# Two layers of a hybrid decoder: page numbers clamped once, and the merged stage planned with other step durations

## The chip, the cores and the metric

The kernel runs on one core of a Trainium2 chip. The metric is the device time of one execution in microseconds (us). A core has TensorE (PE, matmuls), VectorE (DVE), ScalarE (ACT) and GpSimd (POOL), each with its own in-order instruction queue, and SyncE (SP), which computes nothing: its queue issues all DMAs of this kernel. Engines hand work to each other by semaphores that are counted up and waited for.

## The reference

One inference step of two decoder layers, for a prompt of 512 tokens and 8 sample sequences of one new token each with 2048 past tokens in a paged cache. Per layer:

```
h = rms_norm(x); proj = h @ w_in
q, kv_rows, win_rows, gates = nsa_project(proj[..., :NSA_PROJ], pos)     # rotary, sigmoid gates
o_nsa  = gates-weighted sum of three attentions: compressed blocks, top-16 selected blocks of 64, window of 512
o_rwkv = rwkv_time_mix(proj[..., NSA_PROJ:], state)                      # scan S = S*w + (S a) b + v k
x = x + rms_norm(concat(o_nsa, o_rwkv) @ w_out)
x = x + rms_norm(conv_ffn(rms_norm(x)))                                  # up 1024->5632, width-3 conv, gelu, down
```

For the samples, the keys and values of the past come from `cache_kv` through `page_table`: `page_table[b, i]` is the physical page (128 tokens) of logical page i of sequence b, 16 pages per sequence, 160 pages in the pool. Everything is float32.

## The kernel before

Both layers run in one hardware loop (`Fori(0, DEPTH)`) on every engine. A layer has dense parts (w_in at the start; w_out, w_up and w_down at the end), in which 128x1024 weight chunks pass through a ring of three (`ring`, line 740), ACT and DVE split each into a high and a low part (lines 1297 and 1632), and PE multiplies three products per block (lines 826 to 828). Between them lies a short stage for rotary, compression and the samples' RWKV step, and then the *merged stage*, which runs from about 270 to 745 us of layer 1.

The merged stage interleaves three independent jobs: the RWKV scan of the prompt in four super-chunks (`rwkv`), the prompt's attention in 32 units (`att`), and the samples' attention (`sample`). The order is not written by hand. `rwkv_threads`, `att_thread`, `sample_thread` and `load_thread` (lines 158 to 327) list every step with its engine, a duration in us and what it depends on; `placed` (line 330) simulates the engines and puts the steps in one list, choosing the step that can begin first, less a favour for its thread; `merged_order` (line 362) varies the favours at random in 4000 rounds and keeps the order with the shortest simulated span. `HOP` is what a dependence adds, `LANDING` the same for a load. The result is the list `PAIRED` (line 403), and PE, DVE and ACT each walk through that same list and emit their part of each step. An engine's queue is in order, so a step that waits holds up all behind it.

The samples' past comes in 36 *units* per layer through three slots of 1 MB (`load_unit`, lines 688 to 707). Units 0 to 15 are compression rows (8 pages each), 16 and 17 window keys, 18 and 19 window values (one DMA each), 20 to 27 selected keys and 28 to 35 selected values (16 pages each). Unit u may be loaded when PE has used unit u-3 (`u_used`). For each unit SP loads the page numbers from SBUF into registers (line 704, with a check that each lies within the pool), and then issues one DMA per page, with an address worked out from the register (line 707). PE's users of the units are line 1145 (compression), 1176 (window keys, step `win_k`), 1184 (`sel_k`), 1220 (`win_v`) and 1229 (`sel_v`).

At the very start, SP issues consts, pages and x (lines 712 to 714, semaphore `const_ok`), and right behind them the layer's parameters (`par`, shift, lora; lines 732 to 734) and the first three weight chunks. DVE, ACT, PE and POOL wait for `const_ok`. POOL then clears 8192 columns of the arena (line 1559); DVE scales `onesblk` (line 1597), waits for the parameters and scales a part of `par` (line 1643), and after the norm writes `hm` (line 1648).

Of the kernel before, what the change touches and what calls it, by code (L numbers as in the profile page):

```python
# [150 lines left out]
HOP, LANDING = 0.25, 2.5  # L151
# [6 lines left out]
def rwkv_threads():  # L158

    front, back, side, tail = [], [], [], []  # L160
    for sc in range(SEQ // SC):
        def into(thread):
            def put(name, engine, us, *after):
                deps = [("rwkv", sc + a[0], a[1]) for a in after if 0 <= sc + a[0] < SEQ // SC]
                thread.append((("rwkv", sc, name), engine, us, deps))
            return put

        here, ago, next_ = (lambda *names: [(0, n) for n in names]), (lambda n: (-1, n)), (lambda n: (1, n))
        put = into(front)
        put("mix", "DVE", 0.5, ago("rkv"))  # L170
        put("tanh", "ACT", 1.0, *here("mix"))
        put("mixlow", "DVE", 1.8, *here("mix"))
        put("squares", "DVE", 1.5, *here("mixlow"))
        put("lora_w", "PE", 1.7, *here("tanh"))
        put("sigw", "ACT", 1.5, *here("lora_w"))
        put("decay", "DVE", 2.4, *here("sigw"))
        put("lora_a", "PE", 1.7, *here("sigw"))
        put("exps", "ACT", 2.2, *here("decay"))
        put("siga", "ACT", 1.5, *here("lora_a"))
        put("kknorm", "PE", 1.0, *here("squares", "siga"))  # L180
        put("keymix", "DVE", 1.5, *here("kknorm"))
        put("root", "ACT", 0.8, *here("kknorm"))
        put("keys", "DVE", 5.3, *here("root"))

        put = into(back)
        put("scaled", "DVE", 3.1, ago(("solve", 1)), *here("exps", "keys"))
        for c in range(2):
            put(("pairb", c), "PE", 1.4, ago(("state", 1)), ago(("yout", 1)), *here("scaled"))
        put(("maskb", 0), "DVE", 0.7, *here(("pairb", 0)))
        put(("pairk", 0), "PE", 1.4, *here(("maskb", 0)))  # L190
        put(("maskb", 1), "DVE", 0.7, *here(("pairb", 1)))
        put("nmm", "PE", 1.4, ago("ycopy"), *here("scaled"))
        put(("pairk", 1), "PE", 1.4, *here(("maskb", 1)))
        put("w0", "DVE", 1.5, *here("nmm"))
        put("zz", "DVE", 1.8, *here(("maskb", 1)))
        for c in range(2):
            put(("maskk", c), "DVE", 0.7, *here(("pairk", c)))
        for lv in range(1, LEVELS):
            put(("inv", lv), "PE", 1.4, *here(("add", lv - 1) if lv > 1 else "w0", ("maskb", 1)))
            put(("qcopy", lv), "ACT", 0.6, *here(("inv", lv)))  # L200
            put(("dbl", lv), "PE", 2.0 if lv < LEVELS - 1 else 1.0, *here(("qcopy", lv), "zz", ("maskk", 1)))
            put(("add", lv), "DVE", 1.5 if lv < LEVELS - 1 else 0.8, *here(("dbl", lv)))
        for c in range(2):
            put(("rhs", c), "PE", 2.0, *here(("state", 0) if c else ("add", LEVELS - 1), ("tmcopy", 2)))
            put(("rhcopy", c), "ACT", 0.4, *here(("rhs", c)))
            put(("solve", c), "PE", 0.8, *here(("rhcopy", c)))
            put(("ucopy", c), "ACT", 0.4, *here(("solve", c)))
            put(("advance", c), "PE", 1.5, *here(("ucopy", c)))
            put(("state", c), "DVE", 1.2, *here(("advance", c)))
            put(("yout", c), "PE", 1.7, *here(("ucopy", c)))  # L210

        put = into(side)
        put("rkprep", "DVE", 1.5, *here("scaled"))
        for n in range(3):
            put(("tm", n), "PE", 1.3, *([ago("vrec")] if n == 0 else here(("tmcopy", n - 1))), *here("scaled"))
            put(("tmcopy", n), "ACT", 0.6, *here(("tm", n)))
        put("glora", "PE", 1.2, *here(("tmcopy", 2)))
        put("gcopy", "ACT", 0.6, ago("out"), *here("glora"))
        put("rknorm", "PE", 1.1, *here("gcopy", "rkprep"))
        put("rkv", "DVE", 0.7, ago("out"), *here("rknorm"))  # L220
# [4 lines left out]
        put("msub", "DVE", 1.5, *here("mean"))
        put("var", "PE", 1.3, *here("msub"))
        put("vrec", "DVE", 4.2, *here("var"))
        put("vroot", "ACT", 0.8, *here("vrec"))
        put("out", "DVE", 3.5, *here("vroot"))
    return [front, back, side, tail]  # L230


def att_thread():

    out = []
    for t in range(NQ):
        w = t + 1

        def put(n, name, engine, us, *after):
            out.append((("att", n, name), engine, us, [("att",) + a for a in after]))  # L240

        first, last = HEADS * t, HEADS * (t + 1) - 1
        put(t, "cs", "PE", 1.4, *([(first - 1, "evac")] if t else []))
        if t:
            put(first - 1, "values", "PE", 0.2 + 0.35 * t, (first - 1, "evac"))
        put(t, "cmask", "DVE", 1.8, (t, "cs"))
        if t:
            put(t - 1, "heads", "DVE", 0.8, (first - 1, "values"))
        put(t, "cexp", "ACT", 0.6, (t, "cmask"))
        put(t, "cweigh", "DVE", 1.6, (t, "cexp"))  # L250
        put(t, "cturn", "PE", 1.2, (t, "cweigh"))
        put(t, "cdone", "DVE", 1.5, (t, "cturn"))
# [9 lines left out]
    put(last, "values", "PE", 0.2 + 0.35 * w, (last, "evac"))  # L262
    put(NQ - 1, "heads", "DVE", 0.8, (last, "values"))
    return out


def sample_thread():
# [6 lines left out]
    put("qz", 0, "DVE", 1.8)  # L274
    for b in range(DEC):
        for q in range(8):
            put("chunks", (b, q), "PE", 1.1, 2 * b + q // 4)
        for name, engine, us in (("cmp_part", "ACT", 0.7), ("cmp_sum", "DVE", 1.8), ("cmp_tanh", "ACT", 0.5),
                                 ("cmp_h", "DVE", 0.4), ("cmp_out", "PE", 0.9), ("cmp_keep", "DVE", 0.7)):
            put(name, b, engine, us)  # L280
    for name, engine, us in (("c_scores", "PE", 1.5), ("c_max", "DVE", 0.4), ("c_exp", "ACT", 0.6), ("c_weigh", "DVE", 1.0),
                             ("c_same", "PE", 0.8), ("c_impt", "DVE", 0.8), ("c_imp", "PE", 4.2), ("c_top", "DVE", 4.0)):
        put(name, 0, engine, us)
    for h in range(2):
        put("win_new", h, "DVE", 0.3, U_WK + h)
        put("win_k", h, "PE", 1.5, U_WK + h)
    for kind in ("win", "sel"):
        if kind == "sel":
            for h in range(2):
                for b in range(QD):  # L290
                    put("sel_k", QD * h + b, "PE", 0.7, U_SK + QD * h + b)
                put("sel_bias", h, "DVE", 0.8)
            put("sel_new", 0, "PE", 0.6)
        for name, engine, us in (("_max", "DVE", 0.6), ("_max_t", "PE", 0.3), ("_max_r", "DVE", 0.7), ("_max_b", "PE", 0.2),
                                 ("_nm", "DVE", 0.3), ("_exp", "ACT", 1.4), ("_den", "PE", 0.2), ("_rr", "DVE", 1.4)):
# [23 lines left out]
def load_thread(smp):  # L319
# [6 lines left out]
    return [(("load", u, "unit"), "SP", 0.6 * UNIT_DMAS[u] + 0.5, [last_use[u - USLOT]] if u >= USLOT else [])  # L326
# [104 lines left out]
def build(nc, I, O):  # L431
    with ExitStack() as ctx:
# [194 lines left out]
        const_ok = ctx.enter_context(nc.semaphore("const_ok"))  # L627
        ones_ok = ctx.enter_context(nc.semaphore("ones_ok"))
# [59 lines left out]
        def load_unit(eng, kind, l, u):  # L688
# [12 lines left out]
            else:  # L701
# [3 lines left out]
                pages[0:1, first:first + n], engines=[kind], min_val=0, max_val=N_POOL - 1)  # L705
# [5 lines left out]
        def _(sp):  # L711
# [17 lines left out]

            with sp.Fori(0, DEPTH) as l:  # L730
# [860 lines left out]
        def _(dve):  # L1591
# [5 lines left out]
            o.do(v.tensor_scalar(onesblk[:], blk, 1.0 / HD, None, MUL))  # L1597
            with dve.Fori(0, DEPTH) as _l:
# [653 lines left out]
```

## Time and profile before

| what | value |
|---|---|
| median of 3 runs | 2500.74 us (2498.71 to 2502.35) |
| the profiled execution's own time | 2501.68 us |
| its span | 2499.9 us |
| busy share of PE, DVE, ACT, POOL | 84%, 50%, 29%, 7% |
| mean granted PE clock | 0.892 |
| 0 to 270 us | dense w_in, then rotary and the samples' RWKV |
| 270 to 745 us | merged stage of layer 1 |
| 745 to 1249 us | dense w_out, w_up, w_down |
| 1249 to 2500 us | layer 2, merged stage at 1515 to 1991 us |

Times in the profile are us from the span's start unless marked ns. "SPq", "DVEq" and so on are the queues' own instructions, which do not count as busy. The granted clock is 1.0 at PE's higher clock level. In a row of a timeline, what stands in brackets is the engine's idle time before the row and what ended it. In the chain of waits, each piece is what the end of the execution was waiting for at that time.

### The profile page before, as it was taken

What the parts mean: (1) busy time and instruction counts of PE and PEld (TensorE: products, weight loads), DVE (VectorE), ACT (ScalarE), POOL (GpSimd) and SP (SyncE); (2) the same over time, 40 slices, a digit from 0 to 9 for tenths busy, and PEclk for the clock granted to TensorE, in tenths of its full rate; (3) what the DMA queues carried; (4) which work ended last, traced back from release to release, by engine and by line L of the source; (5) the groups of instructions that cost most, each with busy time, mean ns of one, the idle gap of its engine ahead of it and who ended that gap; (6) DMA issues with size and microseconds to landing.
All of it is one profiled execution on the core that took longest, in us unless ns stands there. A gap on an engine that the chain in (4) does not pass through costs nothing.

```text
span 2499.9 us, 56131 instructions
## 1 busy us (share of the span) xinstructions
PE 2088.2 (84%) x22574; PEld 1898.2 (76%) x22574; DVE 1251.8 (50%) x2079; ACT 719.3 (29%) x1336; POOL 165.1 (7%) x233
## 2 busy tenths in 40 slices
PE   6996698887768799999669967988878688999995
PEld 5995687755647699999669856776556477999995
DVE  4223767774743644452332236677757435444523
ACT  3221222332323322242132212323423223222421
POOL 1000120100100010000010001101101000010000
PEclk8988798888989799999879977988888798999997
DMA  3264232122222122223123632322222221222232
GB/s 122 93 138 145 71 100 87 54 71 76 59 82 86 51 93 91 90 84 101 47 79 94 147 127 86 93 80 62 72 74 59 89 71 60 93 93 90 89 93 72
DMA packets 172781, 216.53 MB, mean 87 GB/s; under 512 B 39009, under 2 KB 138594, under 8 KB 171106
## 3 DMA queue, kind: packets, MB, share of 16 engines
q1 hardware_dynamic: 172514, 212.87, 28.5%
q8 instruction: 180, 2.95, 0.5%
q14 instruction: 87, 0.71, 0.1%
HBM read 204.57 MB, written 16.59 MB: 88 GB/s over the span
## 4 chain that ended last, share of the span: by engine, by line
PE 59%; DVE 20%; SPq 11%; issue 6%; ACT 3%; DMA 1%; DVEq 0%; ACTq 0%
PE ps L826 15%; PE ps L828 15%; PE ps L827 15%; SPq L707 7%; SPq L704 3%; PE ps L1145 3%; PE ps L894 1%; DVE arena L1675 1%; DVE smp L1940 1%; PE ps L867 1%; DVE arena L1898 1%; DVE x L2081 1%; DVE arena L1905 1%; DVE hf_lo L1639 1%; PE ps L953 1%
## 5 line engine op out<-in xcount | busy, mean ns | idle before, releaser
L826 PE MATMUL ps<-hm_hi,ring_hi 128*128 128x260 f32 x2432 | 694.8, 286 | 35.7 <-DVE hm_lo L1639 35.7
L828 PE MATMUL ps<-hm_hi,ring_lo 128*128 128x260 f32 x2432 | 692.6, 285 | 0.0
L827 PE MATMUL ps<-hm_lo,ring_hi 128*128 128x260 f32 x2432 | 690.5, 284 | 0.0
L1632 DVE TENSOR_TENSOR ring_lo<-ring,ring_hi 128x1024 fp32r<-128x1024 f32 x200 | 244.8, 1225 | 696.9 <-ACT ring_hi L1297 696.2
L826 PEld LDWEIGHTS ps<-hm_hi,ring_hi 128*128 128x128 f32 x2432 | 464.0, 191 | 39.5 <-issue 39.5
L827 PEld LDWEIGHTS ps<-hm_lo,ring_hi 128*128 128x128 f32 x2432 | 463.6, 191 | 0.0
L828 PEld LDWEIGHTS ps<-hm_hi,ring_lo 128*128 128x128 f32 x2432 | 463.3, 191 | 0.0
L1297 ACT ACTIVATE ring_hi<-ring 128x1024 fp32r<-128x1024 f32 x200 | 211.8, 1060 | 681.3 <-PE ps L828 673.9
L826 PE MATMUL ps<-hf_hi,ring_hi 128*128 128x260 f32 x704 | 202.2, 287 | 8.8 <-DVE hf_lo L1639 8.2
L828 PE MATMUL ps<-hf_hi,ring_lo 128*128 128x260 f32 x704 | 200.7, 285 | 0.0
L827 PE MATMUL ps<-hf_lo,ring_hi 128*128 128x260 f32 x704 | 200.4, 285 | 0.0
L826 PEld LDWEIGHTS ps<-hf_hi,ring_hi 128*128 128x128 f32 x704 | 134.5, 191 | 11.4 <-issue 10.6
L828 PEld LDWEIGHTS ps<-hf_hi,ring_lo 128*128 128x128 f32 x704 | 134.5, 191 | 0.0
L827 PEld LDWEIGHTS ps<-hf_lo,ring_hi 128*128 128x128 f32 x704 | 134.4, 191 | 0.0
L1456 ACT ACTIVATE arena<-ps,arena 128x128 f32<-128x128 f32 (+3 forms) x128 | 66.5, 525 | 174.5 <-DVEq L428 173.8
L1577 POOL TENSOR_TENSOR arena<-arena,cst 128x256 f32<-128x256 f32 x80 | 63.3, 812 | 679.4 <-DVEq L428 475.4
L1462 ACT ACTIVATE arena<-ps 128x256 f32<-128x256 f32 (+3 forms) x64 | 45.2, 707 | 189.6 <-PE ps L1120 188.5
L843 PE MATMUL ps<-arena,ones 128*32 128x130 f32 x512 | 32.7, 353 | 58.5 <-ACT arena L1307 51.5
L1583 POOL COPY arena<-arena 128x2 f32<-128x2 f32 x44 | 28.5, 648 | 786.3 <-ACTq L428 786.3
L1030 PE MATMUL ps<-nsa 64*64 64x64 f32 x1280 | 78.9, 231 | 0.3 <-ACTq L428 0.2
L1030 PEld LDWEIGHTS ps<-nsa 64*64 64x64 f32 x1280 | 71.6, 141 | 8.1 <-issue 6.0
L1120 PE MATMUL ps<-cst,arena 128*128 128x128 f32 x320 | 57.3, 320 | 24.0 <-DVEq L428 23.9
(376 smaller groups left out, 3295.9 us busy)
## 6 DMA issues: line engine op xcount, KB each, us to landing
ring<-in_w SPq DMA_DIRECT2D x202, 512.0 KB, 3.6
arena<-in_kv_cmp SPq DMA_DIRECT2D x96, 128.0 KB, 2.2
extra<-in_kv_cmp SPq DMA_DIRECT2D x80, 128.0 KB, 2.1
slot<-in_kv_cmp SPq DMA_DIRECT2D x80, 128.0 KB, 2.2
out_win_old<-in_win SPq DMA_DIRECT2D x16, 511.0 KB, 9.3
slot<-in_k_sel SPq DMA_DIRECT2D x96, 64.0 KB, 1.9
arena<-in_k_sel SPq DMA_DIRECT2D x96, 64.0 KB, 1.9
extra<-in_v_sel SPq DMA_DIRECT2D x96, 64.0 KB, 1.9
```

What stands on the lines that cost most here:

```text
L704: _, regs = nc.values_load_multi_w_load_instructions(pages[0:1, first:first + n], engines=[kind], min_val=0, max_val=N_POOL - 1)
L707: eng.dma_start(dst[:, i, :], src[l * N_POOL + r]).then_inc(done, 16)
L826: mmul(out, wh, hi[:, k, cols], start=(k == 0), stop=False)
L827: mmul(out, wh, lo[:, k, cols], start=False, stop=False)
L828: last = mmul(out, wl, hi[:, k, cols], start=False, stop=(ci == len(chunks) - 1 and k == k1 - 1))
L1030: last = mmul(ps[r, 0, cj * CH:(cj + 1) * CH], qq[r, c, j, :], zz[r, c, j, :], start=True, stop=True)
L1120: last = nc.tensor.transpose(ps[:, 4 + g, k * P:(k + 1) * P], pp[:, g, k * P:(k + 1) * P], ident)
L1145: last = mmul(out, w1s[:, c, k, :], slot[:, :, c, k, :], start=(k == 0), stop=(k == STRIDE // 2 - 1))
L1297: A(ring_hi[:, n % RING_HI, :], ring[:, n % RING, :], ACT.Copy).then_inc(S["w_hi"], 1)
L1456: o.go(A(pp[:, g, 0:w], ps[:, 4 + g, 0:w], ACT.Exp, bias=nm[:, g:g + 1], accum_out=sums[:, g:g + 1]))
L1577: o.go(g.tensor_tensor(mm[:, lv % 2, c * RJ:(c + 1) * RJ, :], gb[:, c, :, 0, :], m, ALU.mult))
L1632: v.tensor_tensor(ring_lo[:, n % RING, :], r, ring_hi[:, n % RING_HI, :], SUB).then_inc(S["w_lo"], 1)
```

## The change

Three things change. The page numbers are limited to 0..159 by one instruction of DVE at the start, `pages_ok` tells SP so, SP waits for it ahead of the layer loop, and the loads of page numbers go without the check. The planner's step durations, the hop per engine and the load's cost get other values. The instructions of the steps stay as they are; their order is made anew from these values.

```diff
-HOP, LANDING = 0.25, 2.5
+HOP, LANDING = {"PE": 0.13, "DVE": 0.0, "ACT": 0.0}, 2.5
...
-        put("lora_w", "PE", 1.7, *here("tanh"))
+        put("lora_w", "PE", 1.3, *here("tanh"))
...
-            put(("maskb", 0), "DVE", 0.7, *here(("pairb", 0)))
+            put(("maskb", 0), "DVE", 0.84, *here(("pairb", 0)))
...
-            put(("inv", lv), "PE", 1.4, *here(("add", lv - 1) if lv > 1 else "w0", ("maskb", 1)))
-            put(("qcopy", lv), "ACT", 0.6, *here(("inv", lv)))
-            put(("dbl", lv), "PE", 2.0 if lv < LEVELS - 1 else 1.0, *here(("qcopy", lv), "zz", ("maskk", 1)))
-            put(("add", lv), "DVE", 1.5 if lv < LEVELS - 1 else 0.8, *here(("dbl", lv)))
+            put(("inv", lv), "PE", 1.08, *here(("add", lv - 1) if lv > 1 else "w0", ("maskb", 1)))
+            put(("qcopy", lv), "ACT", 0.72, *here(("inv", lv)))
+            put(("dbl", lv), "PE", 2.06 if lv < LEVELS - 1 else 1.05, *here(("qcopy", lv), "zz", ("maskk", 1)))
+            put(("add", lv), "DVE", 1.43 if lv < LEVELS - 1 else 0.85, *here(("dbl", lv)))
...
-        put("out", "DVE", 3.5, *here("vroot"))
+        put("out", "DVE", 4.2, *here("vroot"))
...
-            put(u, "scores", "PE", 0.3 + 0.25 * w, (u - 1, "evac") if u > first else (t, "cdone"))
+            put(u, "scores", "PE", 0.21 + 0.213 * w, (u - 1, "evac") if u > first else (t, "cdone"))
...
-                put(u - 1, "values", "PE", 0.2 + 0.35 * w, (u - 1, "evac"))
-            put(u, "mask", "DVE", 0.8 + 0.25 * w, (u, "scores"))
-            put(u, "exp", "ACT", 1.0 + 0.22 * w, (u, "mask"))
-            put(u, "weigh", "DVE", 0.9 + 0.25 * w, (u, "exp"))
-            put(u, "turn", "PE", 0.1 + 0.36 * w, (u, "weigh"))
-            put(u, "evac", "ACT", 0.3 + 0.22 * w, (u, "turn"))
+                put(u - 1, "values", "PE", 0.5 + 0.17 * w, (u - 1, "evac"))
+            put(u, "mask", "DVE", 0.78 + 0.265 * w, (u, "scores"))
+            put(u, "exp", "ACT", 0.72 + 0.21 * w, (u, "mask"))
+            put(u, "weigh", "DVE", 0.96 + 0.255 * w, (u, "exp"))
+            put(u, "turn", "PE", 0.27 * w, (u, "weigh"))
+            put(u, "evac", "ACT", 0.3 + 0.21 * w, (u, "turn"))
...
-                    put("sel_k", QD * h + b, "PE", 0.7, U_SK + QD * h + b)
+                    put("sel_k", QD * h + b, "PE", 1.45, U_SK + QD * h + b)
...
-    return [(("load", u, "unit"), "SP", 0.6 * UNIT_DMAS[u] + 0.5, [last_use[u - USLOT]] if u >= USLOT else [])
+    return [(("load", u, "unit"), "SP", 0.53 * UNIT_DMAS[u] + 1.1, [last_use[u - USLOT]] if u >= USLOT else [])
...
-    threads = [[(key, engine, us, [(a, LANDING if a[0] == "load" else HOP) for a in after]) for key, engine, us, after in thread]
-               for thread in (*rwkv_threads(), att_thread(), smp, load_thread(smp))]
+    rows = (*rwkv_threads(), att_thread(), smp, load_thread(smp))
+    ran = {key: engine for thread in rows for key, engine, _, _ in thread}
+    threads = [[(key, engine, us, [(a, LANDING if a[0] == "load" else HOP[ran[a]]) for a in after]) for key, engine, us, after in thread]
+               for thread in rows]
...
             _, regs = nc.values_load_multi_w_load_instructions(
-                pages[0:1, first:first + n], engines=[kind], min_val=0, max_val=N_POOL - 1)
+                pages[0:1, first:first + n], engines=[kind], min_val=0, max_val=N_POOL - 1,
+                skip_runtime_bounds_check_because="VectorE limits every entry to the pool before the first is loaded")
...
+            sp.wait_ge(pages_ok, 1)
             with sp.Fori(0, DEPTH) as l:
...
             o.do(v.tensor_scalar(onesblk[:], blk, 1.0 / HD, None, MUL))
+            o.do(v.tensor_scalar(pages[:], pages[:], 0, N_POOL - 1, MAX, ALU.min))
+            o.tell(pages_ok)
             with dve.Fori(0, DEPTH) as _l:
```

The entries left out change in the same manner, by a few tenths of a us each; most PE steps become shorter and most DVE steps longer.

## Rows read from the trace of the kernel before

**Rows 1.** top of the page, span.
```profile
span 2499.9 us, 56131 instructions
```

**Rows 2.** merged stages in stretches: us; busy PE, PEld, DVE, ACT, POOL; clock; DMA share, GB/s.
```profile
270.00:490.00 220.00, 188.09 (x2430) 161.81 (x2431) 160.58 (x323) 66.12 (x166) 34.05 (x26) 0.89 0.27 78
490.00:745.00 255.00, 193.20 (x3165) 143.51 (x3161) 154.04 (x266) 81.68 (x165) 16.27 (x20) 0.86 0.26 72
1515.00:1735.00 220.00, 187.52 (x2415) 161.47 (x2415) 160.57 (x322) 66.12 (x166) 34.18 (x26) 0.89 0.27 78
1735.00:1991.00 256.00, 196.40 (x3181) 148.36 (x3182) 155.77 (x273) 82.26 (x165) 16.95 (x20) 0.84 0.25 72
```

**Rows 3.** chain of waits from 497 to 743 us, shares by line.
```profile
by line: SPq L707 34.5%; issue 19.2%; SPq L704 17.7%; DVE arena L1898 1.9%; PE ps L1229 1.6%; DVE arena L1905 1.4%; DVE arena L1675 1.4%; DVE arena L1857 1.4%; DVE arena L1816 1.1%; PE ps L973 1.1%; PE ps L1062 0.9%; PE ps L1184 0.8%; DMA s
```

**Rows 4.** stretches of 20 us in that stage.
```profile
590.00:610.00 20.00, 14.29 (x222) 11.33 (x220) 4.48 (x9) 4.57 (x11) 0.00 (x0) 0.73 0.31 85
```

**Rows 5.** PE's waits on a DMA, 270 to 745 us: total us, times, longest.
```profile
PE ps L1229 <- DMA extra<-in_v_sel: 11.1, 2, 8.6
PE ps L1229 <- DMA slot<-in_v_sel: 9.3, 2, 4.8
PE ps L1184 <- DMA arena<-in_k_sel: 5.6, 2, 5.0
PE ps L1184 <- DMA extra<-in_k_sel: 5.4, 1, 5.4
PE ps L1184 <- DMA slot<-in_k_sel: 4.4, 1, 4.4
```

**Rows 6.** lines 704 and 707: count, ns least/median/most, first and last start.
```profile
L704 SPq FUSED_REGOPS  x768: 147/147/178, 184.7 to 1974.5; - x192
L704 SPq SEQ_ASSERT  x768: 18/18/37, 184.9 to 1974.7; - x192
...
L707 SPq FUSED_REGOPS  x768: 44/44/124, 186.8 to 1983.0; - x192
L707 SPq DMA_DIRECT2D slot<-in_v_sel x96: 332/333/1223, 633.8 to 1983.1; - x96
```

**Rows 7.** chain from 495 to 520 us: start, us, what.
```profile
512.27 0.15 SPq L704
516.32 0.05 SPq L707
```

**Rows 8.** timeline of SP's queue, DMA issues: start, us, line, tiles, count.
```profile
489.18 0.37 SPq L696 DMA_DIRECT2D extra<-in_vwin  x1
...
688.93 8.54 SPq L707 DMA_DIRECT2D slot<-in_v_sel  x16
702.73 8.85 SPq L707 DMA_DIRECT2D arena<-in_v_sel  x16
```

**Rows 9.** chain from 660 to 745 us.
```profile
668.43 0.98 SPq L704
...
740.87 1.98 PE ps L1229 x32
```

**Rows 10.** timeline of the start, all engines.
```profile
11.40 0.23 DVE L1597 TENSOR_SCALAR onesblk<-cst 128x128 f32<-128x128 f32 x1 [11.40 <-DMA x<-in_x]
...
11.51 6.99 POOL L1559 MEMSET arena<- 128x8192 f32 x1 [10.56 <-DMA x<-in_x]
...
13.07 5.71 DVE L1643 TENSOR_SCALAR par<-par 128x8 f32<-128x8 f32 x1 [1.44 <-DMA arena<-in_lora]
...
23.59 5.46 DVE L1648 SCALAR_TENSOR_TENSOR hm<-x,par,rstd 128x520 f32<-128x520 f32 x8
```

**Rows 11.** timeline of DVE, 466 to 476 us.
```profile
468.02 2.79 DVE L1962 TENSOR_SCALAR arena<-arena,extra 64x127 f32<-64x127 f32 x1
```

**Rows 12.** timeline at the start of layer 2.
```profile
1253.28 0.36 SPq L732 DMA_DIRECT2D par<-in_cols  x1
...
1267.79 5.46 DVE L1648 SCALAR_TENSOR_TENSOR hm<-x,par,rstd 128x520 f32<-128x520 f32 x8
```

More of the change, by code:

```diff
@@ L169, in rwkv_threads @@
         put = into(front)
[L170 to L173, printed above, removed]
-        put("lora_w", "PE", 1.7, *here("tanh"))
[L175 to L183, printed above, removed]
+        put("mix", "DVE", 0.7, ago("rkv"))
+        put("tanh", "ACT", 1.05, *here("mix"))
+        put("mixlow", "DVE", 1.9, *here("mix"))
+        put("squares", "DVE", 1.75, *here("mixlow"))
+        put("lora_w", "PE", 1.3, *here("tanh"))
+        put("sigw", "ACT", 1.27, *here("lora_w"))
@@ L185, in rwkv_threads @@
+        put("decay", "DVE", 2.56, *here("sigw"))
+        put("lora_a", "PE", 1.3, *here("sigw"))
+        put("exps", "ACT", 1.93, *here("decay"))
+        put("siga", "ACT", 1.26, *here("lora_a"))
+        put("kknorm", "PE", 1.06, *here("squares", "siga"))
+        put("keymix", "DVE", 1.57, *here("kknorm"))
+        put("root", "ACT", 0.72, *here("kknorm"))
+        put("keys", "DVE", 5.42, *here("root"))
         put = into(back)
-        put("scaled", "DVE", 3.1, ago(("solve", 1)), *here("exps", "keys"))
+        put("scaled", "DVE", 2.72, ago(("solve", 1)), *here("exps", "keys"))
@@ L187, in rwkv_threads @@
         for c in range(2):
-            put(("pairb", c), "PE", 1.4, ago(("state", 1)), ago(("yout", 1)), *here("scaled"))
-        put(("maskb", 0), "DVE", 0.7, *here(("pairb", 0)))
[L190 to L195, printed above, removed]
+            put(("pairb", c), "PE", 1.1, ago(("state", 1)), ago(("yout", 1)), *here("scaled"))
@@ L196, in rwkv_threads @@
+        put(("maskb", 0), "DVE", 0.84, *here(("pairb", 0)))
+        put(("pairk", 0), "PE", 1.05, *here(("maskb", 0)))
+        put(("maskb", 1), "DVE", 0.84, *here(("pairb", 1)))
+        put("nmm", "PE", 1.05, ago("ycopy"), *here("scaled"))
+        put(("pairk", 1), "PE", 1.05, *here(("maskb", 1)))
+        put("w0", "DVE", 1.57, *here("nmm"))
+        put("zz", "DVE", 1.64, *here(("maskb", 1)))
         for c in range(2):
-            put(("maskk", c), "DVE", 0.7, *here(("pairk", c)))
+            put(("maskk", c), "DVE", 0.84, *here(("pairk", c)))
@@ L207, in rwkv_threads @@
[L207 to L210, printed above, removed]
+            put(("rhs", c), "PE", 1.6, *here(("state", 0) if c else ("add", LEVELS - 1), ("tmcopy", 2)))
+            put(("rhcopy", c), "ACT", 0.5, *here(("rhs", c)))
+            put(("solve", c), "PE", 0.62, *here(("rhcopy", c)))
+            put(("ucopy", c), "ACT", 0.5, *here(("solve", c)))
@@ L212, in rwkv_threads @@
+            put(("advance", c), "PE", 1.15, *here(("ucopy", c)))
+            put(("state", c), "DVE", 1.03, *here(("advance", c)))
+            put(("yout", c), "PE", 1.25, *here(("ucopy", c)))
         put = into(side)
-        put("rkprep", "DVE", 1.5, *here("scaled"))
+        put("rkprep", "DVE", 1.6, *here("scaled"))
         for n in range(3):
-            put(("tm", n), "PE", 1.3, *([ago("vrec")] if n == 0 else here(("tmcopy", n - 1))), *here("scaled"))
-            put(("tmcopy", n), "ACT", 0.6, *here(("tm", n)))
@@ L217, in rwkv_threads @@
[L217 to L220, printed above, removed]
+            put(("tm", n), "PE", 1.08, *([ago("vrec")] if n == 0 else here(("tmcopy", n - 1))), *here("scaled"))
+            put(("tmcopy", n), "ACT", 0.72, *here(("tm", n)))
+        put("glora", "PE", 1.04, *here(("tmcopy", 2)))
+        put("gcopy", "ACT", 0.72, ago("out"), *here("glora"))
@@ L222, in rwkv_threads @@
+        put("rknorm", "PE", 1.06, *here("gcopy", "rkprep"))
+        put("rkv", "DVE", 0.85, ago("out"), *here("rknorm"))
         put = into(tail)
-        put("ycopy", "ACT", 0.6, *here(("yout", 1)))
+        put("ycopy", "ACT", 0.72, *here(("yout", 1)))
         put("mean", "PE", 1.1, next_("root"), *here("ycopy", "rkv"))
[L225 to L228, printed above, removed]
@@ L229, in rwkv_threads @@
-        put("out", "DVE", 3.5, *here("vroot"))
+        put("msub", "DVE", 1.56, *here("mean"))
+        put("var", "PE", 1.06, *here("msub"))
+        put("vrec", "DVE", 4.37, *here("var"))
+        put("vroot", "ACT", 0.75, *here("vrec"))
+        put("out", "DVE", 4.2, *here("vroot"))
     return [front, back, side, tail]
@@ L242, in att_thread @@
         first, last = HEADS * t, HEADS * (t + 1) - 1
-        put(t, "cs", "PE", 1.4, *([(first - 1, "evac")] if t else []))
+        put(t, "cs", "PE", 1.05, *([(first - 1, "evac")] if t else []))
         if t:
-            put(first - 1, "values", "PE", 0.2 + 0.35 * t, (first - 1, "evac"))
-        put(t, "cmask", "DVE", 1.8, (t, "cs"))
+            put(first - 1, "values", "PE", 0.5 + 0.17 * t, (first - 1, "evac"))
+        put(t, "cmask", "DVE", 1.67, (t, "cs"))
         if t:
[L248 to L252, printed above, removed]
+            put(t - 1, "heads", "DVE", 0.84, (first - 1, "values"))
+        put(t, "cexp", "ACT", 0.53, (t, "cmask"))
+        put(t, "cweigh", "DVE", 1.67, (t, "cexp"))
+        put(t, "cturn", "PE", 1.0, (t, "cweigh"))
+        put(t, "cdone", "DVE", 1.43, (t, "cturn"))
         for u in range(first, last + 1):
-            put(u, "scores", "PE", 0.3 + 0.25 * w, (u - 1, "evac") if u > first else (t, "cdone"))
+            put(u, "scores", "PE", 0.21 + 0.213 * w, (u - 1, "evac") if u > first else (t, "cdone"))
             if u > first:
-                put(u - 1, "values", "PE", 0.2 + 0.35 * w, (u - 1, "evac"))
-            put(u, "mask", "DVE", 0.8 + 0.25 * w, (u, "scores"))
-            put(u, "exp", "ACT", 1.0 + 0.22 * w, (u, "mask"))
-            put(u, "weigh", "DVE", 0.9 + 0.25 * w, (u, "exp"))
-            put(u, "turn", "PE", 0.1 + 0.36 * w, (u, "weigh"))
-            put(u, "evac", "ACT", 0.3 + 0.22 * w, (u, "turn"))
-    put(last, "values", "PE", 0.2 + 0.35 * w, (last, "evac"))
-    put(NQ - 1, "heads", "DVE", 0.8, (last, "values"))
+                put(u - 1, "values", "PE", 0.5 + 0.17 * w, (u - 1, "evac"))
[4 more added lines that the diff above has]
+            put(u, "evac", "ACT", 0.3 + 0.21 * w, (u, "turn"))
+    put(last, "values", "PE", 0.5 + 0.17 * w, (last, "evac"))
+    put(NQ - 1, "heads", "DVE", 0.84, (last, "values"))
     return out
@@ L272, in put @@
         out.append((("smp", n, name), engine, us, ([out[-1][0]] if out else []) + [("load", u, "unit") for u in after]))
-    put("qz", 0, "DVE", 1.8)
+    put("qz", 0, "DVE", 2.2)
     for b in range(DEC):
         for q in range(8):
-            put("chunks", (b, q), "PE", 1.1, 2 * b + q // 4)
-        for name, engine, us in (("cmp_part", "ACT", 0.7), ("cmp_sum", "DVE", 1.8), ("cmp_tanh", "ACT", 0.5),
-                                 ("cmp_h", "DVE", 0.4), ("cmp_out", "PE", 0.9), ("cmp_keep", "DVE", 0.7)):
+            put("chunks", (b, q), "PE", 1.08, 2 * b + q // 4)
+        for name, engine, us in (("cmp_part", "ACT", 0.72), ("cmp_sum", "DVE", 2.3), ("cmp_tanh", "ACT", 0.53),
+                                 ("cmp_h", "DVE", 0.57), ("cmp_out", "PE", 0.7), ("cmp_keep", "DVE", 0.63)):
             put(name, b, engine, us)
-    for name, engine, us in (("c_scores", "PE", 1.5), ("c_max", "DVE", 0.4), ("c_exp", "ACT", 0.6), ("c_weigh", "DVE", 1.0),
-                             ("c_same", "PE", 0.8), ("c_impt", "DVE", 0.8), ("c_imp", "PE", 4.2), ("c_top", "DVE", 4.0)):
+    for name, engine, us in (("c_scores", "PE", 2.4), ("c_max", "DVE", 0.44), ("c_exp", "ACT", 0.6), ("c_weigh", "DVE", 1.0),
+                             ("c_same", "PE", 0.8), ("c_impt", "DVE", 0.8), ("c_imp", "PE", 4.3), ("c_top", "DVE", 3.9)):
         put(name, 0, engine, us)
@@ L285, in sample_thread @@
         put("win_new", h, "DVE", 0.3, U_WK + h)
-        put("win_k", h, "PE", 1.5, U_WK + h)
+        put("win_k", h, "PE", 1.05, U_WK + h)
     for kind in ("win", "sel"):
@@ L290, in sample_thread @@
                 for b in range(QD):
-                    put("sel_k", QD * h + b, "PE", 0.7, U_SK + QD * h + b)
+                    put("sel_k", QD * h + b, "PE", 1.45, U_SK + QD * h + b)
                 put("sel_bias", h, "DVE", 0.8)
             put("sel_new", 0, "PE", 0.6)
-        for name, engine, us in (("_max", "DVE", 0.6), ("_max_t", "PE", 0.3), ("_max_r", "DVE", 0.7), ("_max_b", "PE", 0.2),
-                                 ("_nm", "DVE", 0.3), ("_exp", "ACT", 1.4), ("_den", "PE", 0.2), ("_rr", "DVE", 1.4)):
+        for name, engine, us in (("_max", "DVE", 0.57 if kind == "win" else 1.63), ("_max_t", "PE", 0.3), ("_max_r", "DVE", 0.7), ("_max_b", "PE", 0.2),
+                                 ("_nm", "DVE", 0.3), ("_exp", "ACT", 0.95 if kind == "win" else 2.0), ("_den", "PE", 0.3), ("_rr", "DVE", 1.6)):
             put(kind + name, 0, engine, us)
@@ L307, in sample_thread @@
             if kind == "win":
-                put("win_v", h, "PE", 1.8, U_WV + h)
+                put("win_v", h, "PE", 1.05, U_WV + h)
             else:
                 for b in range(QD):
-                    put("sel_v", QD * h + b, "PE", 0.6, U_SV + QD * h + b)
+                    put("sel_v", QD * h + b, "PE", 1.05, U_SV + QD * h + b)
             put(kind + "_vo", h, "ACT", 0.8)
@@ L627, in build @@
         const_ok = ctx.enter_context(nc.semaphore("const_ok"))
+        pages_ok = ctx.enter_context(nc.semaphore("pages_ok"))
         ones_ok = ctx.enter_context(nc.semaphore("ones_ok"))
```

3 lines of the change are left out of this document (removed).

## The prediction

> **What bounds the kernel now.** I first read the page's chain of waits, which names two lines of SyncE (SP), 704 and 707, beside the dense matmul lines. Since SP computes nothing, I then read the stage in which it stands. The table of stretches cuts the merged stage of layer 1 into 220 and 255 us: 475 us, in which PE is busy for 381 us and DVE for 315 [rows 2]. The second stretch does little more PE work than the first and less DVE work, yet takes 35 us longer. Layer 2 repeats this (220 and 256 us, [rows 2]), so I work on one layer and double it. Asked for 497 to 743 us alone, the chain lies on SP for 34.5% + 17.7%, and most of the 19.2% "issue" is gaps between SP's instructions [rows 3]. The 20 us from 590 show the result: DVE busy for 4.5 us [rows 4].
>
> Who waits says the same: PE's waits on a DMA in that stage are five rows (and one of 0.5), 11.1 + 9.3 + 5.6 + 5.4 + 4.4 = 35.8 us, all for in_k_sel and in_v_sel, none for in_kv_cmp [rows 5]. What makes these loads late is not bandwidth but the making of them. Line 704 issues per page a FUSED_REGOPS of 147 ns and a SEQ_ASSERT of 18 ns; line 707 issues the DMA at 333 ns [rows 6]. The 16 checks of a unit run from 512.27 to 516.32: 4.05 us, or 0.253 us a page with gaps [rows 7]. Back to back, units start 702.73 - 688.93 = 13.80 us apart [rows 8]. With three slots SP can't run ahead of this, and the last sel_v is a pure SP chain: the load that starts at 668.43 is followed by four more, and PE gets the last at 740.87 [rows 9].
>
> **The change, part by part.**
>
> *Checks removed (lines 704 to 705).* I take both kinds on line 704 to go, since the address is worked out by line 707's own 44 ns FUSED_REGOPS [rows 6]. A 16-page unit then costs 13.80 - 4.05 = 9.75 us, an 8-page unit 2 us less than now. The 16 compression units of a layer gain nothing: PE never waits for them [rows 5], so SP only waits longer for slots. For the 16 sel units I replay the old order. The sel_k stalls are 5.6 + 5.4 + 4.4 = 15.4 us [rows 5]; each of the eight units gains 4.05 us, 32 in all, so these stalls go and the first sel_v comes 15.4 us sooner. From there the tail is five SP units, from 668.43 to the PE start at 740.87 [rows 9]; it shortens by 5 x 4.05 = 20.2 us and stays about balanced, since PE's own share of those 72.4 us is 72.4 - 20.4 (its sel_v stalls) = 52 us, against 72.4 - 20.2 = 52.2 for SP. Sum: 15.4 + 20.2 = 35.6 us a layer, 71 us for both. Bounds: 18 us a layer, if half the cover turns into waits for DVE, and 42 us, if also the lower TensorE clock after the stalls goes (the last sel_v starts after an idle of 4.8 us and takes 1.98 us in the chain [rows 9]; the granted clock of the stretch is 0.86 [rows 2]). What is late next is PE and DVE in turn, as in the first stretch.
>
> *The order made anew.* The diff changes no instruction of PE, DVE or ACT here, only their order. Summing the planner's own entries over all steps of a layer, PE falls from 409 to about 361 us and DVE rises from 333 to about 348. So the planner took PE as the only scarce engine and now sees two nearly equal ones. The trace speaks for the new numbers: busy time is 381 for PE, which includes its slow-clock parts, and 315 for DVE without the gaps between its dependent instructions [rows 2]. After the first part the stage is 475 - 35.6 = 439 us with PE busy for 381, a density of 0.87; the first stretch alone has 188.1/220 = 0.855 [rows 2]. I take 0.91 for the new order: 381/0.91 = 419, or about 19 us a layer, 38 for both. This is the softest term. Its ends: -10 us a layer (a loss, if the search lands on a worse order) and 42 us (a stage of 397 us, density 0.96). 0.91 is a choice between today's 0.87 and that.
>
> *The clamp and the new wait at the start.* SP now waits before the layer loop for pages_ok, and behind that wait stand par, shift, lora and the first three weight chunks, which today are issued while x is still landing. VectorE can clamp only after const_ok: its first instruction starts at 11.40 [rows 10]. The clamp itself is about 0.2 us, but at 11.51 GpSimd starts its MEMSET of 6.99 us. Today's first small tensor_scalar behind it, on par, takes 5.71 us from 13.07 [rows 10]; and at 468.02 one over 64x127 takes 2.79 us [rows 11]. So I expect the clamp to end with the MEMSET, at 18.5, and par to be issued at 19.0. In layer 2 the normalised hm starts 1267.79 - 1253.28 = 14.5 us after par's issue [rows 12]. That gives 33.5 against today's 23.59 [rows 10]: +9.9 us, once. x may land a microsecond sooner with 2 MB less beside it, so I take +9. If the clamp slips past the MEMSET, par is issued at 12.2, and 26.7 - 23.6 = +3: that is the low end; +11 is the high one. DVE's queue loses nothing, since the par instruction ends at 18.8 today anyway.
>
> The Trainium skill, page "SBUF — State Buffer", section "Who interferes with whom", says why the small instruction should wait: a tensor_scalar whose source and result lie in SBUF may use the port pair that DVE shares with GpSimd, and whoever issues first holds it for the whole instruction. By that rule the clamp (one source, 128 elements) blocks and the sum has +9; by its instruction time alone it would have +3. By that rule, the trace agrees for two other shapes (5.71 and 2.79 us), and no row shows an int32 row on one partition.
>
> **The sum.** Profiled execution 2501.7 (span 2499.9 [rows 1] and 1.8 around it) - 71 - 38 + 9 = 2401.7. That run is 0.9 above the median of the runs, so I predict 2401.
>
> **The rivals.**
> *A: the order gives much.* PE and DVE interleave at 0.96: stage 397 us, 2 x 78 = 156 less, +9: 2354. For it: the 20 us windows without DMA stalls can be nearly full, and fewer idle gaps raise the clock above 0.86 to 0.89. Against it: DVE needs 315 us plus a gap behind each dependent instruction, so both must fit at once.
> *B: the order gives nothing.* Only the checks count, and the new order is within a few us of the old one or loses up to 10 us a layer: 2501 - 71 + 9 = 2439, up to 2459. For it: the search is random and the real hand-offs and clock dips are not in its costs.
> *C: the checks hardly go.* If the 147 ns FUSED_REGOPS is how a page number gets out of the load and only the SEQ_ASSERT goes, a page saves 0.06 us, a unit about 1 us, and a layer some 8 us: 2501 - 16 - 38 + 9 = 2456. Against it: line 707 has a FUSED_REGOPS of its own.
> *D: slower, through the sel loads' start.* The first sel loads need slots that win_k frees; today vwin's second load is issued at 489.18, right behind win_k, 219 us into the stage [rows 8]. From win_k to the end remain 16 x 9.75 + about 9 for the last products = 165 us whatever else is done. An order that puts win_k later than 475 - 165 - 5 = 305 us into the stage makes both layers longer than now, one for one; at 315 us the stage is 480 and the time 2501 + 10 + 9 = 2520. For it: the new costs make loads look cheap. Against it: the planner counts them at 9.6 us a unit, near my 9.75, so it sees this wall too.
>
> **How the numbers follow.** Forecast 0.58, A 0.17, B 0.15, C 0.06, D 0.04. The forecast's terms hardly all lie at one end; each half way to its ends gives about 2370 to 2445, and I hold 2375 to 2430 for its own range. The range takes in most of A and of B: 2360 to 2447 leaves about 0.08 below and 0.12 above. What differs from no change by less than 0.2% (5 us) a measurement of this kernel can't tell. Only D ends slower: 0.04; between D's break-even and the others 0.01 for no difference; 0.95 faster.
>
> **What would show it.** No SEQ_ASSERT, and no FUSED_REGOPS where the page numbers are loaded; v_sel units 9.7 to 9.9 us apart; less than 8 us a layer of PE waits on k_sel and v_sel; merged stages of 410 to 430 us; hm of layer 1 starting at about 32.5 with the clamp taking some 7 us; dense stretches unchanged. Wrong would be: units still above 12 us apart (C), stages of 435 or more with the loads on time (B), SP idle before win_k and a tail of loads after everything else (D), or a clamp of 0.2 us (then 6 us less).

## The result, and the profile after

Median 2444.71 us (2442.37 to 2447.13) against 2501.55 us for the kernel before on the same chip: ratio 0.9775, 95% interval 0.9758 to 0.9792, 57 us faster. I had forecast 2401, 100 us faster, with 2375 to 2430 as the forecast's own range and 2360 to 2447 as the wide one: the time lies 2 us inside the wide range and outside the other. The profiled execution has a span of 2442.3 us against 2499.9 [rows 1].

The chain of waits from 545 to 724 us of the changed kernel, by line (L711 is the line that issues a page's DMA, L707 the load of the page numbers):

```profile
by line: SPq L711 61.8%; issue 18.2%; SPq L707 8.1%; PE ps L1234 1.1%; PE ps L1239 1.1%; DMA slot<-in_v_sel 1.0%; PE ps L1225 0.6%; PE ps L1181 0.6%; DVE arena L1912 0.5%; DVE arena L1905 0.5%; PE ps L1024 0.5%; DVE arena L1868 0.4%; DVE ar
```

In the part behind win_k, SP's share is larger than it was in [rows 3], although a unit costs SP less: 61.8% + 8.1% against 34.5% + 17.7%. The stretches, cut at win_k and at the first dense matmul (layer 1, then layer 2; columns as in [rows 2]):

```profile
275.10:542.00 266.90, 222.01 (x3138) 188.95 (x3139) 207.23 (x390) 87.38 (x206) 36.54 (x32) 0.90 0.23 69
542.00:732.40 190.40, 142.54 (x2495) 104.20 (x2494) 121.84 (x215) 65.98 (x133) 9.64 (x14) 0.92 0.36 105
1487.00:1753.70 266.70, 221.74 (x3135) 188.82 (x3135) 207.25 (x390) 87.35 (x206) 36.52 (x32) 0.90 0.24 69
1753.70:1941.30 187.60, 144.13 (x2497) 105.86 (x2495) 121.88 (x215) 66.02 (x133) 9.64 (x14) 0.92 0.37 106
```

PE's waits on a DMA, 279 to 735 us, are 16 us in all in place of 36 before [rows 5]:

```profile
PE ps L1234 <- DMA slot<-in_v_sel: 5.3, 1, 5.3
PE ps L1189 <- DMA slot<-in_k_sel: 4.5, 2, 3.2
PE ps L1234 <- DMA arena<-in_v_sel: 3.5, 1, 3.5
PE ps L1234 <- DMA extra<-in_v_sel: 1.7, 1, 1.7
PE ps L1189 <- DMA extra<-in_k_sel: 0.7, 2, 0.3
```

All that is left of [rows 6] where the page numbers are loaded is the load itself (count, ns least/median/most, first and last start):

```profile
L707 SPq TENSOR_LOAD <-pages x64: 520/861/980, 192.5 to 1918.0; - x64
```

SP's queue in the timeline: the second vwin load goes out at 543.12, not at 489.18 [rows 8]; from 562.16 to 707.97 lie 14 units of 10.42 us:

```profile
543.12 0.37 SPq L699 DMA_DIRECT2D extra<-in_vwin  x1
548.10 8.74 SPq L711 DMA_DIRECT2D slot<-in_k_sel  x16
562.16 9.14 SPq L711 DMA_DIRECT2D arena<-in_k_sel  x16
...
698.57 8.19 SPq L711 DMA_DIRECT2D extra<-in_v_sel  x16
707.97 9.37 SPq L711 DMA_DIRECT2D slot<-in_v_sel  x16
...
724.49 1.37 SPq L745 DMA_DIRECT2D ring<-in_w  x3
```

The start, which answers to [rows 10]:

```profile
11.21 0.23 DVE L1602 TENSOR_SCALAR onesblk<-cst 128x128 f32<-128x128 f32 x1 [11.21 <-DMA x<-in_x]
...
11.32 6.99 POOL L1564 MEMSET arena<- 128x8192 f32 x1 [10.37 <-DMA x<-in_x]
11.47 6.91 DVE L1603 TENSOR_SCALAR pages<-pages 1x128 int32<-1x128 int32 x1
...
18.72 0.36 SPq L737 DMA_DIRECT2D par<-in_cols  x1
...
32.25 4.12 DVE L1655 SCALAR_TENSOR_TENSOR hm<-x,par,rstd 128x520 f32<-128x520 f32 x6
```

The clamp, 128 integers on one partition, takes 6.91 us and ends 0.07 us after GpSimd's MEMSET. `par` is issued at 18.72, and `hm` starts 8.7 us later than before.

I cut each layer at three places of the trace: the first store of the stage (wkv_s), PE's first win_k, and the first dense matmul behind the stage. All are in us, layer 1 / layer 2:

| | store at | store to win_k | win_k to dense | stage | PE busy in it | DVE busy in it |
|---|---|---|---|---|---|---|
| before | 265.3 | 222.7 / 222.8 | 266.6 / 265.2 | 489.3 / 488.0 | 387.5 / 388.4 | 326.8 / 327.3 |
| changed | 275.1 | 266.9 / 266.7 | 190.5 / 187.6 | 457.3 / 454.3 | 364.5 / 365.9 | 329.1 / 329.1 |

By this measure, which includes the 14 us of hand-over to the dense part, the stages are 32.0 and 33.7 us shorter. The start costs 9.8, the stretch between the stages is 1.7 us shorter and the tail the same: 9.8 - 65.7 - 1.7 + 0.1 = -57.5, which is the difference of the spans (57.6) but for rounding. Less the same 14 us, the changed stage is 443 us by the prediction's measure (475 before).

### The profile page after: what moved, and what is told of

It reads as the page before. It is cut to its first block, busy times and chain, and to the rows that moved or that the text cites. A ratio compares the mean times of both kernels' runs of the same rounds, so it can differ in the third digit from the quotient of the medians.

```text
span 2442.3 us, 54597 instructions
## 1 busy us (share of the span) xinstructions
PE 2041.1 (84%) x22574; PEld 1859.9 (76%) x22574; DVE 1258.5 (52%) x2080; ACT 719.0 (29%) x1336; POOL 156.1 (6%) x233
## 4 chain that ended last, share of the span: by engine, by line
PE 59%; DVE 21%; SPq 9%; issue 5%; ACT 3%; DMA 1%; DVEq 0%; ACTq 0%
PE ps L831 16%; PE ps L833 15%; PE ps L832 15%; SPq L711 8%; PE ps L1150 2%; PE ps L899 1%; DVE hf_lo L1646 1%; SPq L707 1%; DVE arena L1912 1%; PE ps L1125 1%; DVE arena L1905 1%; PE ps L1118 1%; DMA ring<-in_w 1%; PE ps L872 1%; DVE x L2088 1%
## 5 line engine op out<-in xcount | busy, mean ns | idle before, releaser
L1582 POOL TENSOR_TENSOR arena<-arena,cst 128x256 f32<-128x256 f32 x80 | 53.7, 692 | 647.2 <-DVEq L430 422.0
L1035 PEld LDWEIGHTS ps<-nsa 64*64 64x64 f32 x1280 | 69.6, 137 | 15.0 <-ACTq L430 10.1
L1125 PE MATMUL ps<-cst,arena 128*128 128x128 f32 x320 | 51.4, 295 | 22.0 <-DVEq L430 21.3
```

The lines of the kernel that those rows point to most:

```text
L1035: last = mmul(ps[r, 0, cj * CH:(cj + 1) * CH], qq[r, c, j, :], zz[r, c, j, :], start=True, stop=True)
L1125: last = nc.tensor.transpose(ps[:, 4 + g, k * P:(k + 1) * P], pp[:, g, k * P:(k + 1) * P], ident)
L1582: o.go(g.tensor_tensor(mm[:, lv % 2, c * RJ:(c + 1) * RJ, :], gb[:, c, :, 0, :], m, ALU.mult))
```

## The experiments

Each is compared with the kernel before, run on the same chip. The theory after the result: removing the checks gave more than the whole gain, and the new order gives some back, since it places win_k 44 us later. The rival: other waits took the place of the checks, and the order carries the rest.

**e1: the checks alone, with the old order.** Clamp, wait and unchecked loads; the planner's values of before.

```diff
-HOP, LANDING = {"PE": 0.13, "DVE": 0.0, "ACT": 0.0}, 2.5
+HOP, LANDING = 0.25, 2.5
... (and every step duration, and the load cost, as before)
```

> The kernel before with the clamp, the wait on pages_ok and the loads without the check, and the old planner values (old order). Theory 1 (the checks are the whole gain, as the replay of the old order had it): 2501 - 71 + 9 = 2439 us, merged stages about 36 us shorter, so the new order is worth nothing or costs a few us. Theory 2 (other waits take half of the checks' place, and the new order carries the rest of the 57 us): 2501 - 40 + 9 = 2470 us.

Measured: 2432.14 us, ratio 0.9726 (0.9713 to 0.9740): 12.6 us faster than the whole change. Stages 449.7 / 447.5 us, so the checks are worth 39.6 / 40.5 us a layer. The stretches of layer 1, cut at win_k:

```profile
275.80:498.80 223.00, 188.70 (x2399) 162.38 (x2399) 163.43 (x321) 66.13 (x166) 34.22 (x26) 0.88 0.27 82
498.80:725.50 226.70, 186.11 (x3233) 140.77 (x3230) 163.67 (x283) 87.59 (x173) 17.16 (x20) 0.91 0.31 89
```

PE's waits on a DMA over 275 to 760 us fall to 6.9 us:

```profile
PE ps L1232 <- DMA extra<-in_v_sel: 3.3, 1, 3.3
PE ps L1232 <- DMA slot<-in_v_sel: 2.1, 2, 1.3
PE ps L1187 <- DMA arena<-in_k_sel: 1.5, 1, 1.5
```

**e2: the order alone, with the checks.** The changed kernel with the checked loads, without clamp and wait.

```diff
-                skip_runtime_bounds_check_because="VectorE limits every entry to the pool before the first is loaded")
+                )
```

> The new planner values (new order) with the checked loads of before and no clamp. Theory 1 (the new order puts win_k about 264 us into the stage, against 219, and 16 checked units of about 14 us follow it whatever the rest does): stages of 264 + 16 x 14 + 9 = 497 us, 13 to 22 us longer than before, so about 2530 to 2545 us. Theory 2 (the new order is better by itself): faster than before by 2 x 10 us or more, 2480 us or less.

Measured: 2558.16 us, ratio 1.0233 (1.0219 to 1.0247): 58 us *slower* than before. Stages 519.8 / 517.5 us, win_k 269.2 us into the stage, and 250.6 us from there to the dense part. The rival falls: the order carries nothing of the 57 us, and with expensive loads it costs 30 us a layer. By the theory's sum 16 checked units of 14 us and 9 us of products follow win_k, 233 us, and the 14 us of hand-over make it 247; measured are 250.6. This is the wall that I had described as case D, there as a rival to the whole change.

**e3: the wait later.** `sp.wait_ge(pages_ok, 1)` just ahead of the first unit load.

```diff
-            sp.wait_ge(pages_ok, 1)
             with sp.Fori(0, DEPTH) as l:
...
+                sp.wait_ge(pages_ok, 1)
                 for u in range(USLOT):
```

> The changed kernel with the wait on pages_ok moved from ahead of the layer loop to just ahead of the first unit load, so that par, shift, lora and the first weight chunks are issued as before; the clamp stays where it is. Theory 1 (the held-back parameter loads cost the 8.7 us by which the first hm is later): hm again at 23.6 us and 8 to 9 us faster than the changed kernel, 2436 us. Theory 2 (that delay is made up later, since the ring runs ahead of PE): within 2 us of the changed kernel.

Measured: 2440.79 us, ratio 0.9753 (0.9740 to 0.9767). Its interval and the changed kernel's overlap, so this run alone decides nothing. `hm` starts at 24.4 us, 7.9 sooner (theory 1 had 23.6), and the stage starts 8.8 sooner; but its stages are 460.6 / 455.8 us, 3.3 and 1.5 longer than in the changed kernel, with the same order.

**e4 and e5: the selected loads made nearly free for SP**, with the new and the old order. This leaves out the page lookup of these units.

```diff
+            if u >= U_SK:
+                eng.dma_start(dst, src[first:first + n].rearrange("n p t -> p n t")).then_inc(done, 16)
+                return
```

> The changed kernel, but each of the 16 selected-key and selected-value units of a layer is one DMA of 16 consecutive pages in place of 16 DMAs by page number: this leaves out the page lookup of these units, and their data are other pages. It takes SP's 10.4 us a unit away. Theory 1 (behind win_k the stage is a wall of SP's unit loads): the part from win_k to the end shrinks from 182 us to what PE and DVE need, 142/0.9 = 157 us, so 25 us a layer and about 2395 us. Theory 2 (PE and DVE are as late as SP by then): less than 5 us a layer, 2435 us or more.

> The old order with clamp and unchecked loads, and each of the 16 selected-key and selected-value units as one DMA of 16 consecutive pages (leaves out the page lookup of these units). Theory 1 (in the old order PE waits only 7 us a layer for loads once the checks are gone): 3 to 7 us a layer faster than the old order with unchecked loads, 2420 to 2426 us. Theory 2 (SP still sets the end of the stage there): 15 us a layer or more, below 2405 us.

Measured: 2422.65 us (ratio 0.9683, 0.9660 to 0.9707) and 2420.31 us (0.9680, 0.9666 to 0.9695). With the new order, win_k to dense shrinks from 190.5 to 180.9 us, less than half of what I expected; with the old order from 226.7 to 220.2, as theory 1 of e5 had it. Neither theory is met for e4: SP does hold the new order's tail, by 10 us a layer, but something else would hold it at 181 us, where PE is busy for 146.2 us and DVE for 122.1; what that is, no run shows. And with SP out of the way the new order is only as good as the old one: the times agree within their intervals, and its stages are 447.7 / 443.9 against 443.1 / 442.7 us. The order's loss of 7.6 / 6.8 us a layer (the changed kernel against e1) shrinks to 4.6 / 1.2. So the load wall explains about 3 and 6 us of the order's loss, and not why the new durations bring no gain.

**e6: one planner entry, the load's cost.** The changed kernel's own trace shows 10.4 us for a 16-page load, not 9.6:

```diff
-    return [(("load", u, "unit"), "SP", 0.53 * UNIT_DMAS[u] + 1.1, ...
+    return [(("load", u, "unit"), "SP", 0.61 * UNIT_DMAS[u] + 0.6, ...
```

> The changed kernel with one planner value altered: a load costs 0.61 n + 0.6 (10.4 us for 16 pages, as the changed kernel's trace shows; 0.53 n + 1.1 gives 9.6), which gives another order, with win_k about 206 us into the planned stage in place of 245. Theory 1 (the new order loses because its tail from win_k to the end is a wall of loads, which this order starts earlier): stages 15 to 20 us shorter than in the changed kernel, 2405 to 2415 us, and below the old order's 2432. Theory 2 (the other new durations are what make the order worse): no better than 2440 us.

Measured: 2373.41 us, ratio 0.9498 (0.9482 to 0.9514): 71 us faster than the changed kernel by one entry. The stage in two stretches, win_k at 488.20, the clock behind it at 0.95 (0.92 in the changed kernel):

```profile
274.90:488.20 213.30, 181.32 (x2375) 154.56 (x2375) 161.46 (x334) 67.14 (x168) 32.52 (x26) 0.91 0.29 86
488.20:696.80 208.60, 175.79 (x3255) 133.39 (x3255) 158.34 (x270) 86.43 (x171) 13.83 (x20) 0.95 0.34 96
```

Stages are 421.9 / 421.3 us. PE waits 2.9 us for loads in layer 1. The gain is twice what the wall explains: store to win_k fell from 266.9 to 213.3, while win_k to dense grew only from 190.5 to 208.6. A part of it may be GpSimd's (e8): what its instructions take from DVE fell by 9 us a layer. No run takes the two apart.

**e7: another seed of the search**, `default_rng(2)`, values as in the change.

> The changed kernel with the planner's random numbers from seed 2 in place of 0, all values as in the change. Its planned win_k is at 213 us, its planned length 415.6 against 413.9. Theory 1 (the place of win_k decides, and the search leaves it to luck): 2 to 8 us a layer faster than the changed kernel, 2428 to 2440 us, though its own plan is longer. Theory 2 (the planned length tells): 3 us slower, 2448 us.

Measured: 2431.48 us, ratio 0.9723 (0.9707 to 0.9739), with win_k at 228 us and stages of 447.8 / 449.7: an order whose own plan is longer runs 13 us faster.

**e8: GpSimd's long instructions cut.** This leaves out most of the shifted difference.

```diff
-                        o.do(g.tensor_tensor(dif, pr[:, :, lo:lo + SC], pr[:, :, lo + 1:lo + SC + 1], ALU.subtract))
-                        o.go(g.tensor_tensor(dif, dif, wide(C("mu"), SC), ALU.mult))
+                        ... (the same two on the first of 14 tiles, 128x128)
```

> The changed kernel, but GpSimd's two instructions per super-chunk that prepare the shifted difference (128x1792, 3.18 us each, six a layer) work on 128x128 alone: this leaves out most of that difference. Theory 1 (the order is 22 us behind its plan at win_k, in part since DVE's small instructions wait up to 3.2 us for these): DVE's busy time falls by 8 us a layer or more, win_k comes 6 to 12 us sooner, and so does the end, since a wall of loads follows: 2420 to 2432 us. Theory 2 (hidden behind PE): under 3 us a layer, 2439 us or more.

Measured: 2407.06 us, ratio 0.9634 (0.9618 to 0.9651): 38 us faster, more than theory 1 had. DVE's busy time falls by 16.2 us a layer, from 329.1 to 312.9, though DVE's instructions are the same, and win_k comes 21.1 us sooner, 245.8 us into the stage. The planner's own plan had put it at 245 (named above e6's result) and the changed kernel reached it at 266.9, so these instructions are most of what kept the order from its plan up to there. It is not a wait for GpSimd's result: in the changed kernel's stage no wait of DVE, PE or ACT is put down to GpSimd. The stretches of e8, cut at win_k:

```profile
275.10:520.90 245.80, 214.85 (x3135) 181.55 (x3135) 190.48 (x388) 87.60 (x206) 19.59 (x32) 0.95 0.25 75
520.90:710.90 190.00, 146.09 (x2495) 106.79 (x2495) 122.49 (x216) 65.85 (x133) 9.11 (x14) 0.91 0.36 105
```

The long instructions look like this in the changed kernel (timeline of DVE and of GpSimd, 476 to 488 us):

```profile
479.11 3.19 DVE L1909 TENSOR_SCALAR arena<-arena 128x2 f32<-128x2 f32 x1 [0.18 <-DVE arena L1673]
482.33 0.17 DVE L1910 RECIPROCAL arena<-arena 128x2 f32<-128x2 f32 x1
482.53 3.01 DVE L1911 TENSOR_TENSOR arena<-arena,gates 128x2 f32<-128x2 f32 x1
```

```profile
479.09 3.18 POOL L1571 TENSOR_TENSOR arena<-arena 128x1792 f32<-128x1792 f32 x1 [1.44 <-DVEq L430]
482.35 3.17 POOL L1572 TENSOR_TENSOR arena<-arena,par 128x1792 f32<-128x1792 f32 x1
```

A tensor_scalar over 128x2 takes 3.19 us in place of 0.17, and a tensor_tensor over 128x2 takes 3.01: each ends with one of GpSimd's two. The Trainium skill (page "SBUF — State Buffer", section "Who interferes with whom") lists both kinds: a DVE instruction in a two-port mode, which a tensor_scalar can enter, and one with two SBUF inputs beside a GpSimd instruction that reads SBUF. The trace agrees, with 3.19 and 3.01 us. The planner has no thread for GpSimd, so where these three pairs a layer fall is chance. DVE's busy time above 312.9, the value with them cut, measures it: about 14 us a layer before, 16 in the changed kernel, 7 in e6 and 7 in e7. So the old order loses nearly as much DVE time in this way as the new one; the same cut with the old order was not run.

**e10, e11, e12: what adds up, what was luck, what the durations are worth.** e10 is e6 with e3's late wait; e11 is e6 with seed 1; e12 is e1 with the load cost 0.61 n + 0.6.

> The changed kernel with the load cost 0.61 n + 0.6 and with the wait on pages_ok just ahead of the first unit load: the version that the runs so far point to. By the load cost alone 2373 us was measured, by the late wait alone 4 us less than the changed kernel, though the first hm came 8 us sooner. If the two add up: 2365 to 2370 us. If the late wait's gain is lost in how the loads then meet the order: 2372 us or more.

> The changed kernel with the load cost 0.61 n + 0.6 and the planner's random numbers from seed 1. Its plan is 408 us with win_k at 205, that of seed 0 is 409 us with win_k at 206. Theory 1 (the load cost is what made 2373 us, by an early win_k): within 15 us of it, 2360 to 2390 us. Theory 2 (2373 us was one lucky order): back at 2420 us or more.

> The old step durations and hop with the load cost 0.61 n + 0.6 (the old one was 0.6 n + 0.5, nearly the same), the loads unchecked, the clamp in place. Theory 1 (the new step durations are worth something once the load cost is right): about the 2432 us of the old order, 2420 to 2440 us, so the durations carry most of the 59 us down to 2373. Theory 2 (the load cost alone made it): 2390 us or less.

Measured: e10 2363.86 us, ratio 0.9464 (0.9451 to 0.9477), 81 us faster than the changed kernel and the best of all; by the ratios the late wait gives 0.34% or 8.5 us here, which it did not give in e3. e11 2394.12 us (0.9585, 0.9572 to 0.9598), 4 us outside what theory 1 allowed and far from theory 2: the load cost made most of e6's gain, and some 21 us of its gain lay in the one order that seed 0 found. e12 2442.89 us (0.9766, 0.9753 to 0.9780): with the old durations the same load cost brings nothing, it even runs 11 us slower than e1. So with a load cost near the measured one the new step durations are worth 38 to 70 us (2432 or 2443 with the old ones, 2394 or 2373 with the new; e1's own load cost, 10.1 us for 16 pages, is near the measured one too). With 9.6 us they bring nothing (2445 or, by e7's seed, 2431 against e1's 2432). Each setting of the planner has been tried with two seeds at most, the old durations with one at each load cost, and two seeds lie 13 to 21 us apart.

## Why the prediction was right or wrong

- *The time* came out inside the wide range by luck. Two errors partly cancel: removing the checks gave 80 us for both layers where I had 71, and the new order cost 14 where I had a gain of 38. My own signs say the same: PE waits of 16 us in layer 1 (I had under 8), units 10.42 us apart (9.7 to 9.9), a stage of 443 us (410 to 430, and 435 or more named as a sign against me); hm at 32.3 (32.5) and the dense stretches came out.
- *What bounds the kernel* was right: SP's making of the sel loads. The sum for the checks, 35.6 us a layer, measured 39.6 / 40.5 (e1). The replay counted only waits. PE's waits on a DMA fell by some 29 us a layer (36 to 6.9), and PE's own busy time in the stage by 12.7 / 14.0 (387.5 / 388.4 to 374.8 / 374.4), with the same matmuls: less idle time, a clock of 0.91 behind win_k in e1 against 0.86 [rows 2]. That was in my upper bound of 42, not in the value that I took.
- *A unit costs 9.75 us*: it costs 10.42. Most DMA issues take 0.33 us, but about one per unit takes 0.8 to 1.5 us. The rows that I had chosen for the price showed the median of 333 and the most of 1223 ns side by side [rows 6]; the price had to be taken over many units, not one. The pair that I subtracted, 13.80 us apart, was a cheap one: the four distances from 673.95 to 730.72 us of the same trace have a mean of 14.19.
- *The clamp and the start* were right in mechanism and size: the clamp took 6.91 us, par was issued at 18.72 (19.0), hm came 8.7 us later (9). The rule of the Trainium skill that I had put beside it (page "SBUF — State Buffer", section "Who interferes with whom") holds here also for an int32 instruction on one partition, and the trace agrees: 6.91 us.
- *The order made anew* is the step that failed. I took -19 us a layer by a density of 0.91 (my own numbers give 439.4 - 419.0 = 20), with ends of -42 and +10; against e1 the changed kernel is +7.6 / +6.8. The density was a choice that no row supported for an order planned with a load cost of 9.6 us. What the runs show in its place is two things. First, the load wall: win_k moved from 223 to 267 us into the stage, and the loads behind it take 16 x 10.42 = 167 us, where the planner counted 153. With cheap loads for SP, 10 us a layer come back, 3 to 6 more than the old order gets (e4, e5). With the measured cost the search starts the loads early, and the order is then worth 27.8 / 26.2 us a layer against e1 (e6), or 21.4 / 16.8 with another seed (e11): about the size that I had forecast. I had this wall as case D, but asked only whether it made the kernel slower than before, not what it did to my own term. Second, GpSimd: its long instructions stop DVE for up to 3.2 us each and push the whole in-order list back (e8: 20 us a layer, and win_k comes where the plan had it). I had used that very lock for the clamp and did not look for it in the stage. It explains why the new order falls short of its plan; that it makes the new order worse than the old one is not shown, since DVE loses 14 us a layer by it in the old order too.
- *Case B* (the order gives nothing or loses up to 10 us a layer, 2439 to 2459 us) is what came true, at 2445; case D's mechanism is a part of what filled it. A was not tested further; C is refuted by the trace, which has neither kind of check instruction left.
- What stays open: why some 5 of e3's 8.8 us at the start were lost again in longer stages and e10's were not. Stages with the same order differ by 1 to 3 us between e3 and the changed kernel, and between e10 and e6; I did not isolate the cause. Open too is what is left of the order's loss when SP's loads are cheap (4.6 / 1.2 us a layer).

## What to carry to other kernels

An order from a planner is as good as the resource that it prices worst: here one entry, 9.6 in place of 10.4 us for a load, cost 37 to 71 us, by the seed (2445 or 2431 against 2394 or 2373), and better step durations brought nothing until that entry was right. When a change mixes a removed cost with a new schedule, run each alone (e1 and e2 settled it): the headline of 57 us was a gain of about 68 (the checks, less what the clamp costs at the start) and a loss of about 12 (the order). And when an engine's small instructions show a maximum near 20 times their median, look at which other engine's instruction ends with them.

## What the runs showed of the hardware that I had not expected

GpSimd's two 128x1792 instructions of 3.18 us stop DVE's short ones, also those with two SBUF inputs (3.01 us for a tensor_tensor over 128x2), and cutting them to 128x128 took 16.2 us a layer off DVE's busy time and 38 us off the kernel. SP's DMA issues, 0.33 us each, have strays of 0.8 to 1.5 us, 15 of the 239 between 560 and 717 us of the changed kernel, which add up to 13 us: nearly 0.9 us for a 16-page unit.
